# Feed-forward blocks of a hybrid encoder step: three chains of seven-product periods and two plain output pairs become one chain of 28 periods

## The reference, cut to what matters

```python
def swiglu(x, w_in, w_out):
    gate, up = jnp.split(x @ w_in, 2, axis=-1)
    return (jax.nn.silu(gate) * up) @ w_out

x = x + 0.5 * swiglu(rms_norm(x, norm_g[l, 0]), ffn_w_in[l, 0], ffn_w_out[l, 0])
x = x + mixer(rms_norm(x, norm_g[l, 1]))
x = x + 0.5 * swiglu(rms_norm(x, norm_g[l, 2]), ffn_w_in[l, 1], ffn_w_out[l, 1])
```

## Time and profile before

| | before |
|---|---|
| median of 3 runs | 2038.64 us (2036.41 to 2039.73) |
| the profiled execution: its time | 2035.2 us |
| the profiled execution: its span | 2033.4 us |
| TensorE busy | 2002.0 us, 16132 matmuls |
| VectorE busy | 1371.8 us |
| ScalarE busy | 1032.2 us |
| GpSimd busy | 1369.0 us |
| read from HBM | 180.81 MB |

### The profile page before, as it was taken

The page is one execution under the profiler, slowest core; times in us unless marked ns, Lnnn a source line. Parts: engine busy times, 40 slices in busy tenths (PEclk is TensorE's granted clock), DMA queues, the critical chain, the costliest instruction groups (busy, mean ns, idle before and its releaser), DMA issues.

```text
span 2033.4 us, 42098 instructions
## 1 busy us (share of the span) xinstructions
PE 2002.0 (98%) x16132; PEld 1954.0 (96%) x16132; DVE 1371.8 (67%) x2205; ACT 1032.2 (51%) x1983; POOL 1369.0 (67%) x1115
## 2 busy tenths in 40 slices
PE   9999999999999999999999999999999999999998
PEld 8999999999989999999999999999998799999997
DVE  7758666535757866757777585764976678567574
ACT  6656554221574655656356565532432437556551
POOL 6977866654425886885679688665643268868764
PEclk9999999999999999999999999999999999999999
DMA  4222323222112222222222222233210232222222
GB/s 161 104 102 86 104 104 102 89 104 78 62 54 84 84 102 106 96 93 99 88 84 104 104 89 100 105 119 114 89 63 32 91 104 84 104 93 97 103 94 76
DMA packets 34026, 190.86 MB, mean 94 GB/s; under 512 B 4144, under 2 KB 6704, under 8 KB 15408
## 3 DMA queue, kind: packets, MB, share of 16 engines
q1 hardware_dynamic: 26496, 173.43, 24.4%
q10 hardware_dynamic: 7344, 14.89, 2.0%
HBM read 180.81 MB, written 7.50 MB: 93 GB/s over the span
## 4 chain that ended last, share of the span: by engine, by line
PE 75%; POOL 12%; DVE 4%; issue 4%; ACT 3%; DMA 0%; POOLq 0%; ACTq 0%; SPq 0%; DVEq 0%
PE ps L787 44%; PE ps L702 15%; PE ps L717 8%; POOL wl L651 3%; POOL ta L564 3%; POOL ws L570 3%; POOL tf L542 1%; POOL wh L647 1%; PE ps L1017 1%; POOL tf L550 1%; POOL tf L557 1%; PE ps L861 1%; PE ps L1570 1%; DVE a L2440 1%; PE ps L1221 1%
## 5 line engine op out<-in xcount | busy, mean ns | idle before, releaser
L787 PE MATMUL ps<-tt,ws 128*128 128x272 f32 x3840 | 523.7, 289 | 3.4 <-DVE ws L2475 1.7
L787 PEld LDWEIGHTS ps<-tt,ws 128*128 128x128 f32 x3840 | 497.9, 188 | 6.3 <-issue 3.9
L570 POOL TENSOR_TENSOR ws<-wraw,ws 128x512 fp32r<-128x512 f32 x312 | 404.1, 1308 | 64.3 <-ACT ws L1829 47.0
L570 POOL TENSOR_TENSOR ws<-s,ws 128x512 fp32r<-128x512 f32 x208 | 270.6, 1301 | 195.6 <-ACT ws L1867 126.3
L787 PE MATMUL ps<-u,ws 128*128 128x272 f32 x2880 | 400.3, 288 | 0.7 <-DVE tg L2343 0.7
L787 PEld LDWEIGHTS ps<-u,ws 128*128 128x128 f32 x2880 | 376.5, 188 | 1.1 <-POOL ws L570 1.1
L647 POOL TENSOR_SCALAR wh<-wraw 128x1024 fp32r<-128x1024 f32 (+2 forms) x132 | 125.5, 951 | 349.6 <-PE ps L717 211.1
L651 POOL TENSOR_TENSOR wl<-wraw,wh 128x512 fp32r<-128x512 f32 (+1 forms) x255 | 345.6, 1373 | 11.0
L702 PE MATMUL ps<-u,wh 128*128 128x272 f32 x1120 | 187.6, 289 | 2.3 <-POOL wl L651 1.1
L2471 DVE TENSOR_TENSOR s<-ps,wraw 128x512 f32<-128x512 f32 x104 | 71.8, 691 | 166.2 <-POOL ws L570 166.2
L702 PEld LDWEIGHTS ps<-u,wh 128*128 128x128 f32 x1120 | 156.7, 188 | 5.2 <-issue 2.6
(11 more groups left out here) (411 smaller groups left out, 3936.2 us busy)
## 6 DMA issues: line engine op xcount, KB each, us to landing
wraw<-in_wf_in SPq DMA_DIRECT2D x87, 1024.0 KB, 4.8
wraw<-in_wf_out SPq DMA_DIRECT2D x32, 1024.0 KB, 4.7
wraw<-in_wf_out SPq DMA_DIRECT2D x16, 768.0 KB, 4.3
wraw<-in_w_ab SPq DMA_DIRECT2D x12, 1024.0 KB, 4.7
wraw<-in_w_cd SPq DMA_DIRECT2D x10, 1024.0 KB, 4.8
wraw<-in_w_abo SPq DMA_DIRECT2D x8, 512.0 KB, 3.2
wraw<-in_w_cdo SPq DMA_DIRECT2D x8, 512.0 KB, 3.2
wraw<-in_w_bv SPq DMA_DIRECT2D x2, 1024.0 KB, 4.9
```

Of the source, the lines that this page charges most:

```text
L570: return nc.gpsimd.tensor_tensor(wide(p, b, 1), src, wide(p, b, 0).bitcast(F32), ALU.subtract)
L787: last = nc.tensor.matmul(bank(b, 0, HT), ws[weights][w][:, i * P:(i + 1) * P], moving[:, part], start=(start and i == 0 and w == 0 and pa ...
```

## The change

The groups of the hidden width stay, but the input pairs are staged by `INPUTS` = 0 to 9, 10 to 17, 18 to 21. So two input periods of the next group (8 and 9, later 16 and 17) run ahead of the output periods of the group before. All four output pairs of groups 0 and 1 are now periods (`OUT7` = 4). A block is then one chain: input periods 2 to 9, output periods 0 to 3 of group 0, input periods 10 to 17, output periods 0 to 3 of group 1, input periods 18 to 21, and behind it the four plain pairs of group 2 as before. The activations of chunks 8 and 9 (16 and 17) wait in `tg` until the output periods have left the slots of `a`. The sums for the last two chunks of a group are finished one period after the group's last input period but one, in a period that I call closing (i = 9 and 17).

```diff
 GROUPS = [(0, 8), (8, 16), (16, 22)]
+INPUTS = [(0, 10), (10, 18), (18, 22)]
...
-OUT7 = DC // 2 - 1
+OUT7 = DC // 2
...
+            items = []
+            for n, (lo, hi) in enumerate(INPUTS):
+                st = FFN_STAGE[f] + 2 * n
+                items += [(STAGE[st][1] + i - lo, i, DC, False, sum(i >= top for _, top in GROUPS))
+                          for i in range(max(lo, LEAD), hi)]
+                if n < G - 1:
+                    items += [(STAGE[st + 1][1] + j, j, GROUPS[n][1] - GROUPS[n][0], True, n) for j in range(OUT7)]
...
+        STARTS = [lo for lo, _ in GROUPS[1:]]
+        LATE = [lo + d for lo in STARTS for d in range(2)]
...
-            fits = not p.out and (p.i - chunks) % 2 == 0 and p.g < G - 1 and 2 * j >= GROUPS[p.g][0]
-            return j if fits else None
+            fits = not p.out and (p.i - chunks) % 2 == 0 and 0 <= 2 * j < STARTS[-1]
+            return j if fits and not (chunks == 4 and 2 * j + 2 in STARTS) else None
+
+        def closing(p):
+
+            return not p.out and p.i - 1 in STARTS
...
# GpSimd, act_sums: the slot is free once the last output period has read it
+                if 2 * j in STARTS:
+                    gone = last_out(f, 2 * j)
+                    pool.wait_ge(seven_done, sevenths(gone, "P7"))
+                    pool.wait_ge(prod_done[0], gone.c + 1)
...
# GpSimd, period
                     if second is not None:
                         act_low(f, second, 0)
+                    if closing(p):
+                        act_low(f, second, 1)
...
# TensorE, one
+                    if p.out and p.i == 0:
+                        pe.wait_ge(act_ready, FC * f + GROUPS[p.g][1])
...
# TensorE, block
-                for g in range(G):
-                    sevens(f, g)
-                    out, base = st + 2 * g + 1, FC * f + GROUPS[g][0]
-                    if g < G - 1:
-                        first_out(out, base)
-                    elif f == 3:
-                        last_rows(out, base)
-                    else:
-                        run_out(out, base)
+                sevens(f, 0)
+                out, base = st + PARTS - 1, FC * f + GROUPS[-1][0]
+                if f == 3:
+                    last_rows(out, base)
+                else:
+                    run_out(out, base)
...
# ScalarE, period
+                    if last and last.out and not p.out:
+                        act.wait_ge(prod_done[1], p.c)
+                        for i in (p.i - 2, p.i - 1):
+                            glu_high(f, i)
                     snapshot2(p)
+                    if closing(p):
+                        act_highs(second, 1)
                     high_s4(p)
...
-                    if not p.out and p.i > GROUPS[g][0]:
+                    if not p.out and p.i - 1 not in LATE:
                         glu_high(f, p.i - 1)
...
# VectorE, period
-                        if not last.out and last.i > GROUPS[g][0]:
+                        if not last.out and last.i - 1 not in STARTS:
                             glu_low(f, last.i - 1)
...
+                    if last and last.out and not p.out:
+                        glu_low(f, p.i - 2)
```

More of the change, by code:

```diff
@@ L403, in trunk @@
             d = [n - st for st in FFN_STAGE if 0 <= n - st < PARTS]
-            plain += (LEAD, 1, 0, 1, 0, count)[d[0]] if d else count
+            plain += (LEAD, 0, 0, 0, 0, count)[d[0]] if d else count
         SEQ = []
         for f in range(4):
[L409 to L418, removed]
+            items = []
[5 more added lines that the diff above has]
+                    items += [(STAGE[st + 1][1] + j, j, GROUPS[n][1] - GROUPS[n][0], True, n) for j in range(OUT7)]
+            last = len(items) - 1
+            SEQ.append([[Period(c, SEVENS * f + k, i, K, (last - k) % 2, k == last, out, g)
+                         for k, (c, i, K, out, g) in enumerate(items)]])
         PAIR_OF = {(f, p.i): p.c for f in range(4) for chain in SEQ[f] for p in chain if not p.out}
@@ L532, in low_t, with last_out @@
                                         ALU.subtract).then_inc(t3_ready, 1)
+            def last_out(f, lo):
+                return [p for p in SEQ[f][0] if p.out and GROUPS[p.g][1] == lo][-1]
             def act_sums(f, j):
@@ L666, in _ @@
                             low_t(f, i)
[L667 to L673, removed]
-                    act_sum2(f, j)
-                    act_sum4(f, j)
-                    act_low(f, j, 0)
-                    act_low(f, j, 1)
-                else:
-                    for i in range(count):
-                        split(i, (first + i) % 2, i // 2, i % 2, SEQ[f][part // 2][-1] if i == 0 else None)
-                        if (f, part) == (1, PARTS - 1) and i:
-                            low_t(2, i - 1)
+                if part == 0:
+                    seven_lows(f, 0)
+                if part < PARTS - 1:
+                    continue
+                for i in range(count):
+                    split(i, (first + i) % 2, i // 2, i % 2, SEQ[f][0][-1] if i == 0 else None)
+                    if (f, part) == (1, PARTS - 1) and i:
+                        low_t(2, i - 1)
             pool.wait_ge(y_gain, len(POOL_ROWS))
@@ L772, in made @@
                 def made(p, what, i):
-                    if p.out and p is seq[0] and what in (E1, E2, T4, T3):
-                        pe.wait_ge(ta_ready, parts_of(f, GROUPS[g - 1][0] // 2 + i) + (1 if what in (E1, T3) else 2))
+                    if p.out and p.i == 0 and what in (E1, E2, T4, T3):
+                        pe.wait_ge(ta_ready, parts_of(f, GROUPS[p.g][0] // 2 + i) + (1 if what in (E1, T3) else 2))
                     elif p is SEQ[f][0][0] and what in (E1, E2):
@@ L1770, in ffn @@
                     t_highs(f, 2)
-                for g in range(G):
-                    seven_acts(f, g, [lambda: (glu_high(f, 0), gate(1))] if g == 0 else [],
-                               [lambda: t_highs(f, 3)] if g == 0 and f != 2 else [])
+                seven_acts(f, 0, [lambda: (glu_high(f, 0), gate(1))], [lambda: t_highs(f, 3)] if f != 2 else [])
                 if f == 0:
@@ L3273 @@
                       for i in range(4)])
-    wf_out = {f"wf_out{g}": np.stack([np.concatenate([
-        pairs_of(wo[i, lo * P:hi * P], list(range(2)), hi - lo),
-        (sevens_of if g < G - 1 else pairs_of)(wo[i, lo * P:hi * P], list(range(2, DC)), hi - lo)]) for i in range(4)])
+    wf_out = {f"wf_out{g}": np.stack([
+        (sevens_of if g < G - 1 else pairs_of)(wo[i, lo * P:hi * P], list(range(DC)), hi - lo) for i in range(4)])
         for g, (lo, hi) in enumerate(GROUPS)}
```

28 lines of the change are left out of this document (5 added, 23 removed).

## The result

| | before | after |
|---|---|---|
| median of 3 runs, us | 2038.64 | 2020.0 |
| lowest and highest, us | 2036.41, 2039.73 | 2018.14, 2021.63 |
| profiled execution, us (span) | 2035.2 (2033.4) | 2021.63 (2019.8) |
| matmuls | 16132 | 16036 |

What follows compares the result with a forecast made beforehand. TensorE was taken to bound the kernel, a stream of matmuls almost without gaps. Eight seams at 2.20 us give 17.6 us, other costs 0: median 2038.6 - 17.6 = 2021.0 us, range to name 2016.5 to 2027.

Steps and rivals of the forecast that it cites:

- The count and the seam: At each of eight seams, 33.79 us become 31.59 us: 2.20 us less each, 17.6 us in all.
- The window of the first block: First block, first period to last four pairs: 300.45 us become 296.0 us; four blocks gain 17.8 us.
- The two parts: Per seam, 1.51 us from 12 fewer matmuls (12.1 us for all 96) and 0.69 us from waits.
- The closing period: GpSimd gets another low part of 1.38 us, ScalarE a 0.63 us cast ahead of S4's high part; cost 0.
- A12's margin: Behind the closing period, GpSimd's A12 ends 2.0 us later, at 209.7; TensorE wants it at 213.20; about 3.5 us remain.
- S4's: In the closing period, S4 ends at 205.7 and is wanted at 208.69: 3.0 us of margin.
- The first input period behind the outputs: ScalarE's two 0.63 us casts fit in its idle time ahead of the second snapshot; cost 0.
- the longer last period of chain 1: Chain 1's end, 0.22 us longer than chain 3's: product seven waits for ScalarE's second snapshot, behind the cast of `ta`.
- the restart: At the start of chain 2, the matmul pipeline restarts, beside a 0.15 us wait for GpSimd's first low part.
- The rival on GpSimd: Behind the closing period, GpSimd instructions lengthen beside VectorE, 1.5 us over the margin: costs 12 us, 2033.0 us; chance 0.04.
- The rival on the loads: Weight loads come too late, margin falling from 5 to 3 us; with 5.7 us of lateness 2042.6 us; chance 0.03.

Runs made afterwards that it cites:

- the two kernels with more low parts: Changed kernel, GpSimd making A12's low part of output period 0 two or four times more: 2020.93 us and 2042.28 us.
- The kernel without the periods in front: Changed kernel, output periods directly behind their own group's inputs, no input period of the next group ahead of them: 2148.53 us, ratio 1.0544.
- The late loads: Changed kernel, each weight load issued behind product seven of the period two before, or behind product one of the next period: 2052.8 us and 2233.99 us.
- with VectorE's order changed as well: Changed kernel, loads behind product seven, and VectorE's join c12 and its rows ahead of the next period's first sum: 2026.39 us, ratio 0.9945.
- The repeated product: Changed kernel, product one of output period 0 run twice at each seam, count back at 16132 matmuls: 2033.17 us, ratio 0.9978.
- the kernel before with the other order of ScalarE: Kernel before, ScalarE making the second snapshot ahead of the cast of `ta` in a chain's last period: 2038.35 us, ratio 1.0005.
- the changed kernel with the other order of VectorE: Changed kernel, VectorE's join c12 and its rows ahead of the next period's first sum, loads not late: 2019.32 us, ratio 0.9912.

## Why the prediction was right

**The count and the seam.** 17.6 us were summed; the four blocks gave 17.7 us and the runs at equal clock 17.7 us. The window of the first block was forecast at 296.0 us and took 295.97. The two parts, 12.1 and 5.5 us, measured 12.3 and 5.4 us. The median was forecast at 2021.0 us and is 2020.0 us; the forecast added the distance of the old profiled run to its median, which is scatter and nothing of the change. That the median is met within 1.0 us is in part luck: the medians of the kernel before lie between 2036.26 and 2038.67 us in the experiments, those of the changed one at 2020.0 and 2018.49 us.

**The closing period.** Its steps came out nearly to the tenth: A12's margin was said to be 3.5 us and is 3.6 us, S4's was 3.0 us (its low part ends at 120.38, product three starts at 123.41). From A12's low part in the closing period (110.59) to the next one (122.99) GpSimd has 10.9 us of work in 12.4 us; forecast were 11.0 us of work and a delay of 2.0 us, and 12.4 less 10.55 us is 1.85 us. That the margin is real and ends where it was said is shown by the two kernels with more low parts: no cost with two, a cost with four.

**The first input period behind the outputs.** ScalarE in after:

```profile
167.17 1.20 ACT L1814 CAST a<-tg 128x544 fp32r<-128x544 f32 x2 [0.88 <-PE ps L797]
170.19 0.39 ACT L1884 COPY snap<-ps 128x272 f32<-128x272 f32 x1 [1.82 <-PE ps L797]
```

Both casts lie in the idle time ahead of the second snapshot, and 1.82 us of it are left.

**What failed without touching the sum.** Three explanations were off. The prediction laid the longer last period of chain 1 to the snapshot behind the cast of `ta`; that wait is there, but the low parts of the plain pair ended no earlier, and taking it away alone gains nothing. The sum held because both went with the seam. At 125.6 ns a matmul the plain pair itself took 0.31 us too long, for which the prediction names 0.15 us of waiting and the restart, without a size.

The rival on GpSimd laid the longer sum of the earlier trace rows to VectorE working beside it. In the trace VectorE works beside both: beside the sum of 1.26 us it makes a low part `a<-tg,a` (90.14 to 91.62), beside the one of 0.77 us a weight sum from PSUM (108.08 to 108.76). So not whether it works but which operation it has could matter; no run isolates it.

The rival on the loads saw the limit in A11 and product one, with some 3 us left and a need for 5.2 us of lateness to eat a seam's gain. The true path is VectorE's first sum ahead of the join. The margin, 2.7 us, is near the 3 us by luck, since it lies on another road, and the cost of crossing it is far larger, since each period pays and not only each seam: 3 us of delay made the kernel slower than before.

**Expectations of experiments that were off.** The kernel without the periods in front was expected to lose the wait for `ta` alone; the wait of chunk 6 and the half clock more than doubled it. The kernel with four more low parts lost more than product two's wait. The late loads cost 33 and 214 us, not up to 10 and about 180; with VectorE's order changed as well, 6 to 7 us stayed, not up to 4. The snapshot ahead of the cast was expected to gain 1.8 us and gained nothing. The repeated product came out at 2033.17 us, above the 2031 to 2032 us expected, while its blocks came out 12.3 us longer, not 12.0. Why the opening and the mixer's clock differ from execution to execution is open.

## What to carry to other kernels

Price a seam by the whole stretch from a product before it to a product behind it, minus the steady rate times the matmuls: it catches waits that hide one behind the other, which a list of waits by cause does not, and it gave this result to 0.1 us. Interleaving the two kinds of work at a seam pays only as far as the slow helper (here GpSimd's sums) gets its time from work of the next group; without it, in the one arrangement tried, the same count of matmuls cost 110 us over the kernel before. A margin must be followed along each engine's queue, not only along the data: here a load that was 3 us late stopped TensorE through an operation that doesn't use it.

## What the runs showed of the hardware

The granted clock can fall without a long stop of TensorE. In the first mixer it fell to 0.51 in the changed kernel's profile, to 0.68 in the next one of the same kernel, to 0.56 in the kernel before with the other order of ScalarE, and not at all in the changed kernel with the other order of VectorE. In 5 us ahead of that place, TensorE was busy for 4.18 us in all four. The Trainium skill, page "TensorE: Matmul & The Clock Gate", section "A second HAM failure mode: psum-queue depth-cycling", tells of a kernel whose clock goes back and forth since TensorE idles briefly between groups of matmuls; here there is one idle time of 0.8 us ahead of the place, with a fall behind it and without one, so no run here shows that cause. Between the profiles of the changed kernel with and without the fall it makes 2.8 of 3.6 us and 1.4 of 2.1 us; most of the rest is the opening. Behind the long waits of the kernel without the two input periods the clock fell each time: behind 4.0 us of idling, product one took 2.08 to 3.06 us in the eight seams, against 1.67 us, and at the first seam two products ran at 0.50 and 0.52.
